# A decoder layer on one core: page steps, one-hot products and low parts placed differently in the first feed-forward

## The reference

```python
xp = xp + 0.5 * swiglu_ffn(rms_norm(xp, g_ffn1), w_ffn1_in, w_ffn1_out)    # D_MODEL 1024, D_FF 2816
xs = xs + 0.5 * swiglu_ffn(rms_norm(xs, g_ffn1), w_ffn1_in, w_ffn1_out)
# one projection of rms_norm(x): convolution inputs, q, k, v, indexer, gates
# sample attention: index_scores over 4096 cached + 8 new keys, top_k of 256 per query,
logits = jnp.where(admissible, scores, -inf); _, idx = lax.top_k(logits, topk)
k_sel  = pool_k[pt[idx // PAGE_SIZE], idx % PAGE_SIZE]                    # gathered rows of 8 heads x 64
att_s  = softmax(q_s . k_sel) . v_sel
# prompt attention with its own top-k, convolution branch, merge by gates, output projection
x = x + 0.5 * swiglu_ffn(rms_norm(x), w_ffn2_in, w_ffn2_out)
```

## Time and profile before

| | |
|---|---|
| time before, median of 3 runs | 1533.76 us (1533.26 to 1534.85) |
| the profiled execution, its own time | 1530.37 us |
| its span in the trace | 1528.6 us |
| TensorE busy | 1434.3 us (94%) |
| VectorE busy | 1068.6 us (70%) |
| ScalarE busy | 508.0 us (33%) |
| GpSimd busy | 583.1 us (38%) |

### The profile page before, as it was taken

The page is one execution under the profiler, slowest core; times in us unless marked ns, Lnnn a source line. Parts: engine busy times, 40 slices in busy tenths (PEclk is TensorE's granted clock), DMA queues, the critical chain, the costliest instruction groups (busy, mean ns, idle before and its releaser), DMA issues. The chain is left out here.

```text
span 1528.6 us, 20727 instructions
## 1 busy us (share of the span) xinstructions
PE 1434.3 (94%) x8219; PEld 1126.1 (74%) x8219; DVE 1068.6 (70%) x1659; ACT 508.0 (33%) x760; POOL 583.1 (38%) x412
## 2 busy tenths in 40 slices
PE   5998999979999988999989998999998999999998
PEld 2333688857888866446766565689998999999998
DVE  1257798998644898999996997667669756664221
ACT  2332422113632222031112233453364444453111
POOL 2000564434338766634426686323203553420000
PEclk8998999989999999999999999999999999999999
DMA  9995363222226887959437886532322223312222
GB/s 346 381 379 210 99 99 106 90 62 84 70 83 216 288 289 252 333 169 339 139 85 251 270 258 186 162 132 83 126 95 69 84 83 110 98 49 75 84 90 83
DMA packets 156929, 248.75 MB, mean 163 GB/s; under 512 B 11965, under 2 KB 104909, under 8 KB 156571
## 3 DMA queue, kind: packets, MB, share of 16 engines
q1 hardware_dynamic: 131742, 164.22, 33.1%
q0 software_dynamic: 23104, 76.16, 15.9%
q10 hardware_dynamic: 1989, 7.07, 1.2%
HBM read 237.58 MB, written 10.20 MB: 162 GB/s over the span
## 5 line engine op out<-in xcount | busy, mean ns | idle before, releaser
L2752 POOL TENSOR_TENSOR w_lo<-w_raw,w_hi 128x1024 fp32r<-128x1024 f32 x65 | 160.5, 2470 | 258.2 <-ACT w_hi L1339 257.9
L696 PE MATMUL ps<-bh,wqr 128*128 128x288 f32 x936 | 205.3, 295 | 4.1 <-DVE wqr L1918 2.0
L1339 ACT ACTIVATE w_hi<-w_raw 128x1024 fp32r<-128x1024 f32 (+1 forms) x88 | 91.5, 1039 | 273.4 <-PE ps L647 204.3
L2819 POOL DMA_INDIRECT kv<-cache_v,idxT x128 | 139.3, 1088 | 97.4 <-PE ps L1117 49.3
L2807 POOL DMA_INDIRECT kv<-cache_k,idxT x128 | 140.6, 1098 | 83.8 <-DVE kprod L2446 51.0
L696 PEld LDWEIGHTS ps<-bh,wqr 128*128 128x128 f32 x936 | 155.5, 188 | 5.0 <-DVE wqr L1918 3.8
L647 PE MATMUL ps<-h_hi,w_hi 128*128 128x512 f32 x352 | 139.7, 397 | 9.9 <-DVE xT L2252 8.9
L647 PE MATMUL ps<-h_lo,w_hi 128*128 128x512 f32 x352 | 137.7, 391 | 0.0
L647 PE MATMUL ps<-h_hi,w_lo 128*128 128x512 f32 x352 | 137.6, 391 | 0.0
L712 PE MATMUL ps<-a_hi,wqr 128*128 128x288 f32 x704 | 123.1, 296 | 0.0
L1102 PE MATMUL ps<-h,wn 128*128 128x288 f32 x448 | 113.9, 412 | 5.1 <-DVE U_p L2265 1.9
(11 more groups left out here) (499 smaller groups left out, 3163.3 us busy)
## 6 DMA issues: line engine op xcount, KB each, us to landing
w_raw<-w_ffn_in SPq DMA_DIRECT2D x56, 512.0 KB, 12.6
wq<-w_ffn_in SPq DMA_DIRECT2D x40, 512.0 KB, 3.5
wn<-w_in SPq DMA_DIRECT2D x36, 512.0 KB
qb<-q_scratch SPq DMA_DIRECT2D x64, 256.0 KB
ring<-w_ffn_in SPq DMA_DIRECT2D x28, 512.0 KB
...
```

The lines of the kernel that those rows point to most:

```text
L696: mm = pe.matmul(ps[:, bank + m, 0:HALF], w[:, k, m * P:(m + 1) * P], b[:, j, k, :], start=(j in (0, 1, 5) and k == 0 and fst), stop=(k == ...
L1339: act.activation(w_hi[:, slot, 0:n], w_raw[:, slot, 0:n], ACT.Copy).then_inc(S_("hi_ready"), 1)
L2752: pool.tensor_tensor(w_lo[:, slot, 0:n], w_raw[:, slot, 0:n], w_hi[:, slot, 0:n].bitcast(F32), ALU.subtract)\
L2819: pool.indirect_dma_start(kv[:, V_SLOT[j % 3] + a // 2, a % 2, :], None, rows[1], bass.IndirectOffsetOnAxis(ap=idxT[:, j % 2, t:t + 1], ax ...
```

## The change

It changes where work stands, and on which engine; the arithmetic stays.

- **Search.** `out_add(0, 2)` and `out_add(0, 3)` stand between and behind the last rounds of the search instead of inside the selection.
- **Page steps.** The cast `ptf`, the memset and the differences `dpt` go from VectorE to GpSimd (after `lo(5)`), the sixteen copies `dptb` to ScalarE (`page_steps`, in the pass of i = 5).
- **Ranks and one-hots.** TensorE transposes the ranks two units later, after unit 28 instead of 26, `ends_spread` after 29 instead of 27, `new_chosen` after 33 instead of 32. The products `onehots(0)` to `(5)` stand behind each of units 34 to 39 and `(6)`, `(7)` behind 40 and 42; before, they stood behind 33, 35, 36, 38, 39, 40, 42 and 44. ScalarE's `weigh` and VectorE's `prod` and `low_part` are interleaved to match.
- **Rows and keys.** `rows_out` comes after unit 43 instead of 45, the keys start at 45 and are spread one per unit; 26 of them stand before unit 68 instead of 28, and two more stand in the last group, from `UA + 12` on.
- **Low parts.** GpSimd makes the low parts of units 56 to 67 too (eight of 1024 and four of 512 columns), between gathers. VectorE's twelve are gone.

```diff
 
             return 16 * (n // 16) + 4 * (n % 4) + n % 16 // 4
 
-        ROWS_AT = 45
-        KEYS = [v for v, c in ((47, 1), (48, 1), (49, 1), (50, 1), (51, 1), (52, 1), (53, 1), (54, 1), (55, 1), (56, 1), (57, 2), (58, 2), (59, 1), (60, 2),
-                               (61, 1), (62, 2), (63, 1), (64, 2), (65, 1), (66, 1), (67, 3)) for n in range(c)]
+        ROWS_AT = 43
+        KEYS = [v for v in range(45, 59)] + [v for v, c in ((59, 1), (60, 2), (61, 1), (62, 1), (63, 1), (64, 1), (65, 1), (66, 1), (67, 3)) for n in range(c)]
         KEYS += [UA] + [UA + n for n in range(4)] + [UA + 4 + n * 2 // 5 for n in range(10)] + [UA + 9 + n // 2 for n in range(6)]
         KEYS += [UA + 12 + n * 2 // 5 for n in range(10)]
         KEYS += [UA + 16 + n // 4 for n in range(NS - len(KEYS))]
...
-                pe.wait_ge(S_("rank_ready"), 1)
+                pe.wait_ge(S_("rank_ready"), 4)
...
-                        if (i, j) == (4, 2):
+                        if (i, j) == (5, 0):
                             ranks_turn()
-                        if (i, j) == (4, 3):
+                        if (i, j) == (5, 1):
                             ends_spread()
-                        if (i, j) == (6, 0):
+                        if (i, j) == (6, 1):
                             new_chosen()
-                        if (i, j) == (6, 1):
-                            onehots(0)
-                        if (i, j) == (6, 3):
-                            onehots(1)
-                        if (i, j) == (7, 0):
-                            onehots(2)
-                        if (i, j) == (7, 2):
-                            onehots(3)
+                        if (6, 2) <= (i, j) <= (7, 3):
+                            onehots(4 * i + j - 26)
                         if (i, j) == (7, 3):
-                            onehots(4)
                             new_logits()
                 for n, (cg, q) in enumerate(OUT_AT):
                     if q == 0:
...
-                    if t == 1 and n % 2 == 0 and n < 6:
-                        onehots(5 + n // 2)
-                    if (t, n) == (1, 5):
+                    if t == 1 and n in (0, 2):
+                        onehots(6 + n // 2)
+                    if (t, n) == (1, 3):
                         rows_out()
             def mix_sums():
...
+            def page_steps():
+
+                act.wait_ge(S_("rank_ready"), 4)
+                act.wait_ge(S_("rankT_done"), 4)
+                for a in range(4):
+                    for h in range(2):
+                        for b in range(2):
+                            r0, c0 = 32 * a + 16 * h + 8 * b, 64 * a + 32 * b + 16 * h
+                            link(act.activation(dptb[:, r0:r0 + 8, :], dpt[:, c0:c0 + 16].unsqueeze(1).to_broadcast([P, 8, 16]), ACT.Copy))
+                settle()
+                act.sem_inc(S_("rank_ready"), 1)
+
             def weigh(s):
...
-            search(27, 31)
+            search(27, 29)
+            out_add(0, 2)
+            search(29, 31)
+            out_add(0, 3)
             lk(dve.tensor_tensor(x_, cur, flip, ALU.bitwise_xor))
             thr = x_.bitcast(F32)
-            out_add(0, 2)
 
             link(dve.tensor_scalar(SEL[:, :], S[:, :], thr, 0.0, ALU.is_gt, ALU.add, accum_out=cnts[:, 0:1]))
             lk(count(thr, ALU.is_equal, cnts[:, 1:2]))
...
             link(dve.tensor_tensor(bd[:, :, :], ident[:, :].unsqueeze(2).to_broadcast([P, P, 16]), cend[:, :].unsqueeze(1).to_broadcast([P, P, 16]), ALU.mult))
-            lk(dve.tensor_copy(ptf[:, :], ptb[:, :]))
-            lk(dve.memset(dpt[:, :], 0.0))
             seqs = ptf[:, :].rearrange("p (s n) -> p s n", s=NSEQ)
-            lk(dve.tensor_tensor(dpt[:, :].rearrange("p (s n) -> p s n", s=NSEQ)[:, :, 0:NPAGE - 1], seqs[:, :, 1:NPAGE], seqs[:, :, 0:NPAGE - 1], ALU.subtract))
 
             for c4 in range(4):
                 dve.wait_ge(S_("rankT_done"), c4 + 1)
                 dve.tensor_scalar(RTi[:, 4 * c4:4 * c4 + 4, :], ps[:, 4 + c4, :].rearrange("p (c n) -> p c n", c=4), -1.0, None, ALU.add).then_inc(S_("ranks_taken"), 1)
             dve.wait_ge(S_("ranks_taken"), 4)
-            for a in range(4):
-                for h in range(2):
-                    for b in range(2):
-                        r0, c0 = 32 * a + 16 * h + 8 * b, 64 * a + 32 * b + 16 * h
-                        link(dve.tensor_copy(dptb[:, r0:r0 + 8, :], dpt[:, c0:c0 + 16].unsqueeze(1).to_broadcast([P, 8, 16])))
-            settle()
+            low_part(4)
             lk(dve.tensor_scalar(tmpi[:, :, :], RTi[:, :, :], 4, None, ALU.arith_shift_right))
-            prod(4)
             dve.wait_ge(S_("ends_done"), 1)
             lk(dve.tensor_copy(adig[:, :, :], tmpi[:, :, :]))
             lk(dve.tensor_scalar(tmpi[:, :, :], RTi[:, :, :], 15, None, ALU.bitwise_and))
-            low_part(4)
             lk(dve.tensor_copy(bdig[:, :, :], tmpi[:, :, :]))
+            dve.wait_ge(S_("rank_ready"), 5)
 
             ends = ps[:, 4:8, :].rearrange("p c (r l) -> p (c r) l", l=16)
             for c in range(2):
@@ -2370,6 +2367,8 @@
                     lk(dve.scalar_tensor_tensor(out=pgp[:, :, :], in0=ends[:, 64 * n:64 * n + 64], scalar=jslot[:, c:c + 1], in1=dptb[:, 64 * n:64 * n + 64],
                                                 op0=ALU.is_le, op1=ALU.mult))
                     lk(dve.tensor_reduce(prl[:, c, 64 * n:64 * n + 64], pgp[:, :, :], AX.X, ALU.add))
+                if c == 0:
+                    prod(5)
             dve.sem_inc(S_("ranks_taken"), 1)
             first = seqs[:, :, 0:1].to_broadcast([P, NSEQ, 8])
             for c in range(2):
@@ -2401,33 +2400,30 @@
                         ins.then_inc(S_("onehot_cut"), 1)
 
             onehot(0)
-            prod(5)
+            low_part(5)
             onehot(1)
-            low_part(5)
             onehot(2)
             prod(6)
             onehot(3)
             low_part(6)
             onehot(4)
+            onehot(5)
             dve.wait_ge(S_("ends_done"), 2)
             link(dve.tensor_scalar(nb[:, :], ps[0:NS, 7, 0:NS], -1.0, -OFF, ALU.add, ALU.mult))
             lk(dve.tensor_reduce(small[0:NS, 6:7], ps[0:NS, 7, 0:NS], AX.X, ALU.add))
             lk(dve.tensor_scalar(small[0:NS, 7:8], small[0:NS, 6:7], -1.0, float(TOPK_S), ALU.mult, ALU.add))
             link(dve.tensor_scalar(slotbias[:, :], slotno[:, :], small[0:NS, 7:8], OFF, ALU.is_ge, ALU.mult))
             settle()
...
-            onehot(5)
             prod(7)
             take_own(0)
             low_part(7)
             onehot(6)
             onehot(7)
-            out_add(1, 0)
             dve.wait_ge(S_("row_tile_done"), 2)
             dve.tensor_tensor(nlog[:, :, :], ps[0:NS, 4, :].rearrange("p (h n) -> p h n", h=H),
                               nb[:, :].unsqueeze(1).to_broadcast([NS, H, NS]), ALU.add).then_inc(S_("X_ready"), 1)
-            out_add(1, 1)
+            out_add(1, 0)
             take_own(1)
-            out_add(1, 2)
             dve.wait_ge(S_("ends_done"), 3)
             row = ps[:, 4, 0:P].rearrange("p (s h q) -> p s h q", s=NSEQ, h=2)
             for c in range(2):
...
-                if v + 2 == in_unit(10):
-                    dve.wait_ge(S_("lo_ready"), in_unit(10) + 2)
                 if v == out_unit(2) - 1:
                     prod(10)
-                if in_unit(10) <= v + 2 < UA:
-                    split_lo(v + 2, v % 2, usize(v + 2))
-                if v == out_end(1, 3):
-                    out_add(1, 3)
+                for cg in range(1, 4):
+                    if v == max(out_end(1, cg), ROWS_AT + 1):
+                        out_add(1, cg)
                 if in_unit(8) <= v < in_unit(10) and v % 4 == 3:
                     prod((v - in_unit(8)) // 4 + 8)
...
 
-            for u in range(2, in_unit(10)):
+            for u in range(2, UA):
                 lo(u)
+                if u == 5:
+                    seqs = ptf[:, :].rearrange("p (s n) -> p s n", s=NSEQ)
+                    pool.wait_ge(S_("tab_in"), 16 * 6)
+                    pool.memset(dpt[:, :], 0.0).then_inc(S_("rank_ready"), 1)
+                    pool.tensor_copy(ptf[:, :], ptb[:, :]).then_inc(S_("rank_ready"), 1)
+                    pool.wait_ge(S_("rank_ready"), 2)
+                    pool.tensor_tensor(dpt[:, :].rearrange("p (s n) -> p s n", s=NSEQ)[:, :, 0:NPAGE - 1], seqs[:, :, 1:NPAGE], seqs[:, :, 0:NPAGE - 1], ALU.subtract)\
+                        .then_inc(S_("rank_ready"), 1)
                 if 4 <= u < 4 + KC:
                     pool.dma_start(wconv[:, u - 4, :], inp["w_dw"][0, :, (u - 4) * P:(u - 3) * P].rearrange("w p -> p w"), allow_slow_non_contiguous=True)\
                         .then_inc(S_("gain_in"), 16)
```

22 lines of the change are left out of this document (11 added, 11 removed).

## The result

The changed kernel is slower, by 0.6%: 1540.84 us median (1536.76 to 1549.84, 8 runs) against 1533.60 us (1528.94 to 1538.29, 8 runs) for the kernel before in the same series; ratio 1.0059, 95% interval [1.0038, 1.0081]. That is 9 us more at the ratio, where 6 us less was forecast.

A forecast was written before the change was run, and what follows sets the result against it. TensorE, busy 94% of the span, was taken as the bound. Of 28.8 us to win, new waits and lower clock took 19.0 and late keys 3.7, leaving 6.1: 1533.76 to 1527.7 us, range 1521.0 to 1536.0.

The forecast's parts named there:

- Ranks: Behind unit 28, TensorE waits 2.2 us (0 to 4) for ranks ready at 331.3, VectorE meeting one and a quarter low parts.
- Low parts: VectorE loses 12.5 us of work; GpSimd keeps up in whole units, with waits of 0.3, 2.4 and 1.0 us near the end.
- The 8.85 us go: Search term: TensorE's wait ahead of unit 26 for out_add(0, 3), 8.85 us, disappears because that out_add now comes earlier.
- The predicted 2.3 us at unit 26: Search term: the later scan on VectorE delays GpSimd's low part 26, so TensorE waits 2.3 us, between 0 and 4.6.
- Page steps: Copies moved to ScalarE, cast to GpSimd: no cost to TensorE; 3 us were ScalarE twice as slow.
- One-hots: TensorE waits 0.8 and 0.6 us for onehots(0) and (1), and a new 4.0 us for onehots(6) behind unit 40.
- `wn` was waited for: First native load, behind unit 67: a wait of 1.9 us, its load starting when unit 66 frees the buffer.
- Keys: Two more late keys cost VectorE 5.2 us, of which 3.7 reach TensorE.
- (c): Rival: GpSimd becomes the bound from unit 45 on, giving 1533.7 to 1540.6 us; chance 0.22, of which 0.12 slower.
- (d): Rival: gain taken back at one place, by later selection, ScalarE's copies or late keys: 1534.0 us, no change; chance 0.20.

The follow-up runs named there:

- the twins: The kernel before and the changed kernel, both unchanged, run on one chip: ratios to before 1.0002 and 1.0054.
- search_only: The kernel before with only out_add(0, 2) and out_add(0, 3) moved into and behind the search: ratio to before 1.0028.
- vl_ranks: The changed kernel with VectorE making low parts of units 56 to 67, ranks_turn behind unit 29 and ends_spread behind 30: ratio to before 0.9994.
- again: The changed kernel run once more, unchanged: ratio to the kernel before 1.0073.
- vector_lows: The changed kernel with VectorE making the low parts of units 56 to 67 again: ratio to the kernel before 0.9972.
- paced: The changed kernel with GpSimd's gathers behind low part 67 held to three keys under way instead of six: ratio to before 1.0119.
- hold_sums: The changed kernel with GpSimd stopping ahead of the gather of key 30 until TensorE's sums are there: ratio to before 1.0038.
- paced5: The changed kernel with the gathers behind low part 67 held to five keys under way instead of six: ratio to before 1.0043.
- vl_shift: vl_ranks with new_chosen, the one-hot products and rows_out later too: ratio to the kernel before 0.9986.
- mask_after: The changed kernel with only the copy of newmask moved behind the product CUM: ratio to the kernel before 1.0031.

## Why the prediction was wrong

Two steps failed: the size of the *Ranks* term, and *Low parts*, where the moved work was priced only by whether each low part is in time. By the twins the first belongs to a miss of 4.0 us up to the sums, and the second to one of 7.4 us from there to the end of `probs_turn`.

**Search and ranks: the first step that failed.** "The 8.85 us go" was priced as a gain, with 2.2 us and at most 4 coming back for the ranks. `search_only` shows 13.87 us coming back one unit on, and `vl_ranks` moves the wait on again, to 5.51 us ahead of `onehots(0)` and 2.46 ahead of unit 29. The wait was the place where a late chain was met, not the price of an `out_add`. The forecast moved the ranks from 327.0 to 331.3 us; they were ready at 333.43 + 2.36 = 335.8. The selection began 5.4 us later (305.10 against 299.67) where 1.5 was forecast, 2.2 of it by the first collision, and two more collisions followed. In the changed kernel 7.2 us are left as a wait, outside the stated 0 to 4: the sum had one and a quarter collision, the trace has three, and the small instructions carry them. The predicted 2.3 us at unit 26 did not come: its low part ran from 308.14 in 2.40 us, and the scan began only at 310.08. So at this place the sum is 2.7 us off (7.2 + 0 against 2.2 + 2.3).

**Page steps: right.** The sixteen copies took ScalarE 3.33 us and nothing waited for them. The cast and what stands with it cost VectorE 3.2 us, not "as much again" as 4.41; nothing in the sum hangs on it.

**One-hots: right.** 1.40 and 0.37 us ahead of the first two (0.8 + 0.6 forecast), 3.98 ahead of `onehots(6)` (4.0), the clock at 0.81 behind it (under 0.8 forecast):

```profile
427.00:436.00 9.00, 8.11 (x53) 7.25 (x54) 2.00 (x12) 1.78 (x2) 2.34 (x1) 0.81 0.20 60
```

**Low parts, as far as TensorE's waits for them go: about right.** `again` has 0.48, 1.72 and 2.24 us at units 63, 64 and 66, the twin 0.47, 1.73 and 2.22, against 0.3 + 2.4 + 1.0 forecast. `wn` was waited for 2.2 us in the first profile, and 1.0 and 0.7 in the twin (1.9 forecast).

**Low parts, what else GpSimd does: left out.** This is the second failure, and the larger. The forecast weighed 5.3 us of GpSimd against 5.44 of TensorE and asked only whether the low parts come in time. Behind the last of them gathers were due, and GpSimd sent them in a block that ended between 603.5 and 606.2 us. In the twins, on one chip, VectorE's step behind the sums then came 2.6 us later than before, instead of 5.8 us earlier; in the other three profiles of the changed kernel it came 4.3 to 5.5 us later than in the first profile of before. The sum has no term for this. Taking the low parts back ends it (`vector_lows` beside `again`), and in that series the ratio falls by 0.7 to 1.0%. That the block of gathers, and not something else that goes with the low parts, holds TensorE's signals is argued from the times alone: `paced` and `hold_sums`, which were to test it, ran on quieter chips, and on the chip of `hold_sums` the version with its gathers left in was not held either. On a slower chip, `paced5` left the delay at 8.5 us. So the cause of the delay stays open; shown is that it comes with the low parts on GpSimd, on the slower chips.

**Keys: about right in size, and wrong in what it meets.** Two more late keys cost 5.2 us by the forecast. From the step to the second `U_p` the twins have 142.9 and 147.1 us, 4.2 apart, and `vl_shift` 146.1. Since VectorE's step came late, nothing of the 5.8 us that TensorE had won was left: the `U_p` is 6.8 us later.

**The sum.** Up to the sums, forecast 9.8 us won, measured 5.8 (twins). From there to the end of `probs_turn`, forecast 3.7 lost, measured 11.1: 770.50 in the twin of before, 775.84 after. That makes 5.3 us lost at that point. The ratio of the twins asks for 8 us; the profiles have more, 15.7 (the profiled execution of after was the longest of its ten), of which 8.4 fall between `probs_turn` and the prompt's last products (1004.96 and 1018.70), where TensorE waits longer for ScalarE's `pTp`:

```profile
PE ps L1265 <- ACT pTp L1784: 5.5, 3, 3.9
```

```profile
PE ps L1257 <- ACT pTp L1788: 12.0, 6, 6.4
```

That stretch is 234 to 245 us long in all profiles of the slower chips and 221 to 225 on the two quieter ones, and 239 in `search_only` too, so I can't say how much of it is the change; it stays open. So is why the loss on the quieter chips (`hold_sums`, `mask_after`, 0.3 to 0.4%) is about as large with the gathers held as without.

**Which rival it was.** None as stated. Nearest is (c), GpSimd as the bound, but not by its stated sign of w_lo waits in every unit: units 48 to 62 ran without any wait in the twin. GpSimd was late in its other work. (d) had the later selection, at 4 us instead of 7.2, and by its own sum no change.
